# Half-wide levels in a triangular solve, and two groups of heads half a level apart

## The reference

```
x = x + 0.5 * swiglu(rms_norm(x), w1, w3, w2)          # D_FF = 2816
h = rms_norm(x);  p_rw, p_cv, p_mla, p_gate = split(h @ w_in)
x = x + (sum_i sigmoid(p_gate_i) * branch_i) @ w_o
x = x + 0.5 * swiglu(rms_norm(x), ...)
```

```
sa    = einsum('dbhvk,dbhk->dbhv', state, a_t)
state = state * w_t + sa * b_t + v_t * k_t
out_t = einsum('dbhvk,dbhk->dbhv', state, r_t)
```

## Time and profile before

| | |
|---|---|
| median of 3 runs | 1642.8 us (1632.86 to 1642.88) |
| the profiled execution | 1646.6 us |
| its span | 1644.7 us |
| PE busy | 1560.4 us, 95% |
| PEld busy | 1444.8 us, 88% |
| DVE busy | 1174.0 us, 71% |
| ACT busy | 760.6 us, 46% |
| POOL busy | 90.1 us, 5% |
| mean granted TensorE clock | 0.982 |
| z products (line 979) | 1280 records, 46.8 us busy |
| subtractions (line 1993) | 40 instructions, 47.2 us busy |

### The profile page before, as it was taken

One profiled execution on the slowest core, in us unless ns is written; L12 is line 12 of the kernel. 1 busy time (PEld: TensorE's weight loads), 2 busy tenths in 40 slices (PEclk: granted clock), 3 DMA queues, 4 the chain that ended last, 5 costly groups with the idle time before them and its releaser, 6 DMA issues.

```text
span 1644.7 us, 40178 instructions
## 1 busy us (share of the span) xinstructions
PE 1560.4 (95%) x17083; PEld 1444.8 (88%) x17083; DVE 1174.0 (71%) x1739; ACT 760.6 (46%) x1169; POOL 90.1 (5%) x103
## 2 busy tenths in 40 slices
PE   6999999998898999999999999999989989999999
PEld 6999897777788899999899999868788888999998
DVE  4777776787886576777666766769887765777764
ACT  5444564465161345444444445545721613554442
POOL 1000120000030001000100001200000300010000
PEclk9999999899999999999999999989998999999999
DMA  5855542232011345655556555323320213566554
GB/s 179 274 181 182 190 141 90 78 116 78 17 61 47 104 154 169 194 185 185 191 197 230 185 187 179 116 65 116 103 67 16 73 35 103 156 182 193 187 183 153
DMA packets 61940, 227.92 MB, mean 139 GB/s; under 512 B 6896, under 2 KB 7920, under 8 KB 60880
## 3 DMA queue, kind: packets, MB, share of 16 engines
q1 hardware_dynamic: 60624, 218.26, 41.1%
q0 software_dynamic: 1152, 7.21, 1.2%
HBM read 224.69 MB, written 1.05 MB: 137 GB/s over the span
## 4 chain that ended last, share of the span: by engine, by line
PE 76%; DVE 13%; ACT 5%; issue 3%; DMA 2%; ACTq 0%; SPq 0%; DVEq 0%; POOLq 0%
PE banks L568 16%; PE banks L570 15%; PE banks L569 15%; PE banks L634 10%; PE banks L635 5%; DVE wlo L1516 3%; PE banks L979 2%; DVE cvx L1766 2%; DMA raw<-in_stream 2%; ACT whi L1139 2%; DVE arena L1993 1%; PE banks L860 1%; ACT arena L1334 1%; PE banks L746 1%; PE banks L991 1%
## 5 line engine op out<-in xcount | busy, mean ns | idle before, releaser
L1516 DVE TENSOR_TENSOR wlo<-raw,whi 128x1024 fp32r<-128x1024 f32 x411 | 506.4, 1235 | 298.9 <-ACT whi L1139 297.6
L1139 ACT CAST whi<-raw 128x1024 fp32r<-128x1024 f32 x411 | 429.4, 1048 | 465.4 <-PE banks L570 318.9
L568 PE MATMUL banks<-hx,whi 128*128 128x256 f32 x1696 | 487.0, 287 | 21.3 <-DVE wlo L1516 17.4
L569 PE MATMUL banks<-hx,whi 128*128 128x256 f32 x1696 | 481.3, 284 | 0.0
L570 PE MATMUL banks<-hx,wlo 128*128 128x256 f32 x1696 | 481.2, 284 | 0.0
L568 PEld LDWEIGHTS banks<-hx,whi 128*128 128x128 f32 x1696 | 326.7, 193 | 28.3 <-DVE wlo L1516 16.8
L569 PEld LDWEIGHTS banks<-hx,whi 128*128 128x128 f32 x1696 | 326.9, 193 | 0.2
L570 PEld LDWEIGHTS banks<-hx,wlo 128*128 128x128 f32 x1696 | 326.8, 193 | 0.0
L634 PE MATMUL banks<-gg,whi 128*128 128x512 f32 x704 | 244.3, 390 | 0.0
L568 PE MATMUL banks<-h,whi 128*128 128x256 f32 x760 | 230.5, 303 | 9.9 <-ACT arena L1237 5.4
L569 PE MATMUL banks<-h,whi 128*128 128x256 f32 x760 | 219.4, 289 | 0.0
(11 more groups left out here) (298 smaller groups left out, 1912.5 us busy)
## 6 DMA issues: line engine op xcount, KB each, us to landing
raw<-in_stream SPq DMA_DIRECT2D x411, 512.0 KB, 3.5
arena<-in_wuq POOLq DMA_DIRECT2D x2, 1152.0 KB, 11.7
lo_w<-in_lora POOLq DMA_DIRECT2D x2, 1024.0 KB, 7.9
arena<-in_wukv POOLq DMA_DIRECT2D x2, 1024.0 KB, 14.9
xT<-in_x SPq DMA_DIRECT2D x1, 1024.0 KB, 4.9
out<-xT SPq DMA_DIRECT2D x8, 128.0 KB, 3.4
consts<-in_cst SPq DMA_DIRECT2D x1, 642.5 KB, 8.4
masks<-in_msk POOLq DMA_DIRECT2D x1, 288.0 KB, 4.0
```

What stands on the lines that cost most here:

```text
L568: TE.matmul(o, wh, hi, start=first, stop=False, **kw)
L569: TE.matmul(o, wh, lo, start=False, stop=False, **kw)
L1139: SE.copy(whi[:, m % HL, :], raw[:, m % RAW, :]).then_inc(hi_ready, 1)
L1516: TT(wlo[:, m % HL, :], raw[:, m % RAW, :], whi[:, m % HL, :].bitcast(F), ALU.subtract)\
```

## The change

In every level one of the two diagonal halves of each block of M stays as it is, so only every other run of `s = 2 ** lv` columns is computed. `wing(a, s, b)` is that half of the columns. M and its transpose are now sorted by what they are (`mn[:, 0]` is M, `mn[:, 1]` its transpose, whatever the chunk's parity), so each operation takes 32 columns in place of 64 as its moving side and its output, while the stationary side keeps 64. As `zz` is also used whole, its other half must be zero: POOL clears it, and then clears the old half after each level. ScalarE writes the identity into the halves of `mn` that VectorE no longer masks. On TensorE and VectorE group 1 runs half a level behind group 0, and the four taps are split in two pairs.

```diff
+        HALF_C = C // 2
+        def wing(a, s, b):
+            return a.rearrange("p (n b s) -> p n b s", b=2, s=s)[:, :, b, :]
+        def wings(d, q, s):
...
+            return pair.rearrange("p i (n b s) -> p i n b s", b=2, s=s)[:, :, :, 0, :]
...
+            def clear_zz(d):                                   # GpSimd
+                pool.wait_ge(*ten.at(("turned pairs", d, 1)))
+                settled(pool)
+                for q in QUADS:
+                    other = zz[:, 4 * q:4 * q + 4].rearrange("p x t (n b s) -> p (x t n) b s", b=2, s=2)[:, :, 1 - d, :]
+                    nc.gpsimd.memset(other, 0.0).then_inc(*poo.mark(("zz cleared", d, q, 1)))
+                for lv in range(1, LEVELS - 1):
+                    for q in QUADS:
+                        pool.wait_ge(*ten.at(("mz", d, q, lv)))
+                        settled(pool)
...
+                        nc.gpsimd.memset(old[:, :, 1 - d, d, :], 0.0).then_inc(*poo.mark(("zz cleared", d, q, lv + 1)))
...
                 nc.gpsimd.memset(upad[:, :, HALF + S:], 0.0).then_inc(*poo.mark("pad right"))
+                clear_zz(0)
...
+                clear_zz(1)                                    # behind the convolution's last parts
                 norm(2)
...
+                    def z_products(q, lv):                     # TensorE
+                        s = 2 ** lv
+                        pe.wait_ge(*vec.at(("g2", d, 1) if lv == 1 and q == 0 else ("mn", d, q, lv - 1)))
+                        settled(pe)
+                        for x, t, i, e, f in both:
+                            o = (x * NT + t) * HALF_C
+                            m = TE.matmul(bank[3 * q][f, o:o + HALF_C].rearrange("p (n s) -> p n s", s=s),
+                                          g1[e, 4 * q + x, t, 0, :], wing(mn[e, 0, 4 * q + x, t, :], s, d),
+                                          start=True, stop=True)
+                        m.then_inc(*ten.mark(("z", d, q, lv)))
+                    def mz_products(q, lv):
+                        s = 2 ** lv
+                        pe.wait_ge(*poo.at(("zz cleared", d, q, lv)))
+                        pe.wait_ge(*vec.at(("z", d, q, lv)))
...
+                                TE.matmul(bank[3 * q + 1][e, o].rearrange("p (n s) -> p n s", s=s), m_t, wing(z_, s, d),
+                                          start=True, stop=True)
+                            m = TE.matmul(bank[3 * q + 2][f, o].rearrange("p (n s) -> p n s", s=s), z_, wing(m_t, s, 1 - d),
+                                          start=True, stop=True)
...
                     for lv in range(1, LEVELS):
+                        z_products(0, lv)
+                        if lv > 1:
+                            mz_products(1, lv - 1)
+                        mz_products(0, lv)
+                        z_products(1, lv)
                         fr.at(("level", d, lv))
...
                     for q in QUADS:
+                        if q:
+                            mz_products(1, LEVELS - 1)
...
                     fr.at(("tk", d))                           # ScalarE
+                    for i in range(2):
+                        b = (1 - d, d)[i]
+                        m = SE.copy(mn[:, i].rearrange("p x t (n b) -> p (x t) n b", b=2)[:, :, :, b],
+                                    cc("ident64", C).rearrange("p (n b) -> p n b", b=2)[:, :, b].unsqueeze(1)
+                                    .broadcast_to([P, H * NT, HALF_C]))
+                    m.then_inc(*act.mark(("eye", d)))
...
+                    def zz_masked(q, lv):                      # VectorE
...
+                        ve.wait_ge(*ten.at(("z", d, q, lv)))
+                        TT(zz[:, 4 * q:4 * q + 4].rearrange("p x t (n b s) -> p (x t) n b s", b=2, s=s)[:, :, :, d, :],
+                           bank[3 * q][:, 0:S].rearrange("p (x n s) -> p x n s", n=HALF_C // s, s=s), mask, ALU.mult)\
+                            .then_inc(*vec.mark(("z", d, q, lv)))
+                    def mn_reduced(q, lv):
+                        s = 2 ** lv
+                        m4 = wings(d, q, s)
+                        p4 = banks[:, 3 * q + 1:3 * q + 3, 0:S].rearrange("p i (n s) -> p i n s", s=s)
+                        if lv == LEVELS - 1:
+                            m4, p4 = m4[:, 1], p4[:, 1]
+                        ve.wait_ge(*ten.at(("mz", d, q, lv)))
+                        TT(m4, m4, p4, ALU.subtract).then_inc(*vec.mark(("mn", d, q, lv)))
                     for lv in range(1, LEVELS):
+                        zz_masked(0, lv)
+                        if lv > 1:
+                            mn_reduced(1, lv - 1)
                         if d == 0:
-                            conv(4)
+                            conv(2)
...
+                        mn_reduced(0, lv)
+                        zz_masked(1, lv)
+                        if d == 0:
+                            conv(2)
                         fr.at(("level", d, lv))
+                    mn_reduced(1, LEVELS - 1)
```

More of the change, by code:

```diff
@@ L171, in constants @@
             if n == 0:
[L172 removed]
+                m1[:, d, 0], m1[:, d, 1] = two(-1.0 * m), two(-1.0 * m.T)
             else:
@@ L395, in program @@
         zz = view(M0 + 6 * Q1, H, NT, C)
+        HALF_C = C // 2
+        def wing(a, s, b):
+            return a.rearrange("p (n b s) -> p n b s", b=2, s=s)[:, :, b, :]
+        def wings(d, q, s):
+            n, one = H * NT * C, 4 * NT * C
+            m, m_t = (0, s) if d == 0 else (s, 0)
+            at = MN + q * one + m
+            pair = arena[:, at:at + 2 * (n + m_t - m)].rearrange("p (i n) -> p i n", i=2)[:, :, 0:one]
+            return pair.rearrange("p i (n b s) -> p i n b s", b=2, s=s)[:, :, :, 0, :]
         ys = view(M0 + 7 * Q1, H, NT, HD)
@@ L963, in _ @@
                             b_, k_k = bt[r:r + HD, j, t * P + e * C:t * P + (e + 1) * C], kr4[r:r + HD, j, t, 1 - e, :]
-                            w = bank[4 + x % 4 // 2][:, S * e + o:S * e + o + C]
+                            w, w_t = (bank[4 + x % 4 // 2][:, n + o:n + o + C] for n in (0, S))
                             TE.matmul(w[HD * e:HD * e + HD, :], k_k, b_, start=True, stop=True)
-                            m = TE.matmul(w[HD - HD * e:P - HD * e, :], b_, k_k, start=True, stop=True)
+                            m = TE.matmul(w_t[HD - HD * e:P - HD * e, :], b_, k_k, start=True, stop=True)
                         m.then_inc(*ten.mark(("turned pairs", d, q)))
@@ L973, in _ @@
                             for x in range(4) for t in range(NT) for i in range(2)]
-                    for lv in range(1, LEVELS):
[L975 to L981, removed]
-                        fr.at(("level", d, lv))
[L983 to L993, removed]
@@ L1016, in _ @@
                                     m = TE.matmul(bank[3 * q + 2][e, (x % 4 * NT + t) * C:(x % 4 * NT + t + 1) * C],
-                                                  mn[f, i, x, t, :], gv[f, x, t, :], start=True, stop=True)
+                                                  mn[f, 1, x, t, :], gv[f, x, t, :], start=True, stop=True)
                         m.then_inc(*ten.mark(("y", d, q)))
@@ L1957, in _ @@
                         ve.wait_ge(*ten.at(("turned pairs", d, q)))
[L1958 to L1963, removed]
+                        for i in range(2):
+                            b = (d, 1 - d)[i]
+                            TT(mn[:, i, quad].rearrange("p (e j) t (n b) -> p e (j t) n b", e=2, b=2)[:, :, :, :, b],
+                               banks[:, 4:6, i * S:(i + 1) * S].rearrange("p e (x n b) -> p e x n b", n=HALF_C, b=2)[:, :, :, :, b],
+                               m1[:, i].rearrange("p (n b) -> p n b", b=2)[:, :, b].unsqueeze(1).unsqueeze(1)
+                               .broadcast_to([P, 2, 4, HALF_C]), ALU.mult).then_inc(*vec.mark(("m%d" % i, d, q)))
                         TT(g2[:, quad].rearrange("p x t i n -> p x t (i n)"),
```

32 lines of the change are left out of this document (16 added, 16 removed).

## The result

The changed kernel is slower: median 1649.6 us of 16 runs (1638.7 to 1660.3) against 1638.8 us for the kernel before (16 runs, 1629.5 to 1646.4), ratio 1.0064 with a 95% interval of 1.0038 to 1.0091. That is 10.8 us more, where 9.8 less were forecast, and just outside the range of 1614 to 1648.

A forecast was written before the change was run, and what follows sets the result against it. TensorE-VectorE alternation and TensorE's instruction supply bound the solves. Packet pace -7.8, m0 and m1 masks -2.2, identity copies +0.6 give -9.4 on 1646.6: 1637.2, less 3.8 to the median: 1633 us; range 1614 to 1648.

The forecast's parts named there:

- What bounds the kernel: Four triangular solves, 132.4 us: TensorE and VectorE alternate, with TensorE's instruction supply a second bound at 4.25 us a packet.
- VectorE's prices: Solve masks at 0.42 us for 0.69, subtractions at 0.69 for 1.22, priced by elements without a stride charge.
- POOL: Added memsets in each direction, at most 0.6 us each, hidden: price 0, upper end 6 us.
- The two identity copies a direction: ScalarE's added 128x512 copies at 0.59 us, mostly hidden; 0.6 us added in all.
- The order: In the solves one group's mask and subtraction run under the other's products: 26.6 us less if nothing else limits.
- The layout: One middle level of a first-direction solve drawn from the rows: 4.5 us, not 6.0 to 6.7; solve 24.6 for 31.9.
- rival D: Solves stay at 4.25 us a packet and the half-level offset only moves the waits: 1641 us, chance 0.15.
- The pace: Instruction packets in the solves come 4.0 us apart instead of 4.25, over 31.2 packets: 7.8 us less.
- Matmuls: TensorE's solve products: same number, moving side 32 columns for 64, step still 59 ns, so no gain.
- The other end: The alternative matmul price, a 33 ns step at 32 columns: some 3.5 us more off the four solves.
- Rival C: Half the columns count as less TensorE work, so more solve stretches fall to half clock: 1655 us, slower, chance 0.11.
- Rival B: Instruction fetches don't hold the solves' new order back, so the full savings come through: 1614 us, chance 0.22.

The follow-up runs named there:

- the padded kernel: The changed kernel plus 30 unread 128x256 matmuls on TensorE behind the first group's z products of level 1: 1642.7 us, ratio 1.0010.

## Why the prediction was wrong

- **What bounds the kernel: right.** Supply of instructions and alternation with VectorE were the two bounds of the solves, as the stop in the earlier trace rows and the packets in the earlier trace rows had it. Removing half the instructions took some 20 us off the half-wide kernels, whose alternation is short, and only 4.5 off the kernel before, whose alternation is long.
- **VectorE's prices: right** (0.42 and 0.69 us, no charge for the stride). **POOL: right**: 32 clears of 0.21 us and 8 of 0.33, and TensorE waited for none. The two identity copies a direction took 0.70 us each for 0.59.
- **The order: right in size, wrong in its cause.** The layout gives 105.8 us for the solves if nothing else limits; measured were 105.9 where nothing did, with a level at 4.45 us for 4.5. But the prediction puts that down to one group's mask and subtraction running under the other's products. In step, without the offset, it was 106.9. What shortened the solves was VectorE's narrower work, and the part of rival D that says that the offset only moves the waits was right.
- **The pace: close.** 4.0 us a packet, so 124.8 us, was forecast; with 64 columns and level 1 in step it was 126.6, 4.06 a packet, with 3 us of half clock in it. In the three kernels with 64 moving columns most of the forecast of 0.6% less came through, or half of it (0.30%, 0.48% and 0.51% less).
- **The failed step is "Matmuls", priced as no gain and no cost.** As a duration that was right: at full clock 31 z records take 0.93 us with 32 columns and with 64. (The other end that it names, 3.5 us less, is not worked out there, and nothing of it came.) The Trainium skill ("TensorE: Matmul & The Clock Gate", section LDWEIGHTS) prices a load by its own columns alone, which the edit leaves at 64. These rows agree with it:

```profile
1242.78 0.93 PE banks L1010 x31
```

```profile
1228.50 0.93 PE banks L1017 x31
```

  (the changed kernel's third solve, then that with 64 columns and level 1 in step). But the same edit took the clock: the solves spent about 65 of 139 us at half clock, for 3.4 of 132 before. So "no cost" was false. By the table the narrow moving side costs 0.9% in the changed order, where the whole change was to bring 0.6%.
- **Rival C was what happened:** with half the columns more stretches of the solves fell to half clock. Why they do, its "work counts as less", fits the runs but is not shown by them. It gave 1655 us, 12 above the median shown then; the measured difference is 10.8. Its price for a level at half clock, 8.2 us, was 7.9 (z of levels 2 and 3 in the first solve start at 412.26 and 420.17). That its sum came so close is partly luck: it puts the other levels at 6.2 us, and the one at full clock in the third solve took 5.0. I gave it 0.11 because "the new order leaves less idle time". That argued from busy time, and busy time alone turned out the wrong measure: some full-width stretches at 46% to 52% busy kept the clock, narrow ones at 60% to 67% lost it, and one at 100% didn't regain it in 30 us. A row that sets busy time beside the clock was there (busy for 49%), but only at one width.
- **Rival B fell,** as the fetches do bind. By the rule of the Trainium skill ("Runtime: NRT & Kernel Launch", section Instruction fetch mechanics) they should be mostly hidden; in the solves they are not (stops of 0.43 to 1.16 us in the chain above), and the measurement decides.
- **The range** ended at 1648, as C was counted among what may be left out. A rival with a mechanism, a row and a price near the range's edge should have been in it.

What stays open: the wide products also write twice as much to the banks, so the moving side and the output were not told apart, and how the chip weighs either is not known from these runs. That the full-width kernels lose the clock at some places and keep it at others with the same busy time is not explained. Between the pairs' shorter masks and the rest nothing was separated, and 4.6 us less ahead of the first solve in the profiled execution are not explained. The best version that computes everything keeps the half-wide operations of VectorE and 64 moving columns, in step: 1630.9 us, 0.51% below the kernel before; with level 1 alone in step it is 0.48%, which can't be told apart.

## What to carry to other kernels

Narrowing the moving side of small matmuls can save nothing on TensorE, as here, and it can cost the clock. Check the granted clock of the stretch, not only the busy share, before and after, and where the full width takes no longer, leave it wide. Where many small matmuls stand together, count instructions against the packets of the instruction queue; stops without a releaser that end some 2.5 us after a packet were the sign here. And cut a change in its parts early: here one part (VectorE's width, with the clears and copies that it needs) was worth 0.5%, another (TensorE's width) cost 0.7% to 1.9%, and the third (the offset) gained only while the clock was low.

## What the hardware showed that I had not expected

- 64x64 matmuls with 32 moving columns kept TensorE busy for 30.7 us on end at half clock without its return; with 64 columns the clock came back after 3 to 7 us, and was up all through some stretches with half as much busy time.
- The spread from run to run goes along with this clock: 12 runs of the padded kernel go from 1634.3 us at 0.984 to 1652.5 at 0.969 with the same program.
- Packets of about 253 TensorE instructions came 3.3 to 4.5 us apart where TensorE stopped for them; halving the number of instructions took 20 us off 1633.
